# Rounded x and its remainder side by side in the gated feed-forward, and an inverse in halves instead of quarters

## What is computed

```
h   = rms_norm(x, gain)                 # x * gain / sqrt(mean(x^2) + eps), per token
x   = x + 0.5 * (silu(h @ w_gate) * (h @ w_up)) @ w_out      # 1024 -> 2 x 2816 -> 1024
```

```
u = depthwise_conv3(h @ w_up);  x = x + g2 * (silu(u_gate) * u_val) @ w_down
```

## Time and profile before

| | us |
|---|---|
| median of 3 runs | 2930.77 (2929.78 to 2937.19) |
| profiled execution, time | 2935.89 |
| profiled execution, span | 2934.0 |
| PE busy | 2444.5 (83%) |
| PE weight loads busy | 2122.1 (72%) |
| DVE busy | 1165.4 (40%) |
| ACT busy | 1122.3 (38%) |
| POOL busy | 1242.2 (42%) |

### The profile page before, as it was taken

One profiled execution on the slowest core, in us unless ns is written; L12 is line 12 of the kernel. 1 busy time (PEld: TensorE's weight loads), 2 busy tenths in 40 slices (PEclk: granted clock), 3 DMA queues, 4 the chain that ended last, 5 costly groups with the idle time before them and its releaser, 6 DMA issues. The chain is left out here.

```text
span 2934.0 us, 42793 instructions
## 1 busy us (share of the span) xinstructions
PE 2444.5 (83%) x18163; PEld 2122.1 (72%) x18163; DVE 1165.4 (40%) x2067; ACT 1122.3 (38%) x1495; POOL 1242.2 (42%) x356
## 2 busy tenths in 40 slices
PE   5998968877898998977967899699957776887878
PEld 4997845375898998854456799567746556787878
DVE  2112664332210111665242211266756664334990
ACT  4433422434442443322334443456832221533333
POOL 2874510051775775610033577332211110774655
PEclk8999968987999999977987999899967777898998
DMA  4554401431553553500333354321000000553432
GB/s 138 187 175 123 144 1 44 132 125 46 172 180 124 171 182 118 173 29 12 121 113 101 110 180 143 126 76 58 29 1 1 1 1 17 171 172 115 143 123 94
DMA packets 298691, 305.98 MB, mean 104 GB/s; under 512 B 7249, under 2 KB 294461, under 8 KB 298493
## 3 DMA queue, kind: packets, MB, share of 16 engines
q1 hardware_dynamic: 298493, 303.16, 32.1%
HBM read 302.09 MB, written 1.05 MB: 103 GB/s over the span
## 5 line engine op out<-in xcount | busy, mean ns | idle before, releaser
L363 POOL TENSOR_TENSOR slab_lo<-ring,slab_hi 128x2048 fp32r<-128x2048 f32 (+1 forms) x242 | 1096.5, 4540 | 1045.8 <-ACT slab_hi L354 1045.8
L354 ACT CAST slab_hi<-ring 128x2048 fp32r<-128x2048 f32 (+1 forms) x242 | 451.1, 1868 | 639.8 <-PE bank L386 573.4
L384 PE MATMUL bank<-ffn_h_hi,slab_hi 128*128 128x256 f32 x1408 | 403.1, 286 | 24.0 <-DVE ffn_h_lo L426 24.0
L385 PE MATMUL bank<-ffn_h_lo,slab_hi 128*128 128x256 f32 x1408 | 402.2, 286 | 0.0
L386 PE MATMUL bank<-ffn_h_hi,slab_lo 128*128 128x256 f32 x1408 | 402.1, 286 | 0.0
L384 PEld LDWEIGHTS bank<-ffn_h_hi,slab_hi 128*128 128x128 f32 x1408 | 274.5, 195 | 27.2 <-issue 27.2
L385 PEld LDWEIGHTS bank<-ffn_h_lo,slab_hi 128*128 128x128 f32 x1408 | 274.4, 195 | 0.0
L386 PEld LDWEIGHTS bank<-ffn_h_hi,slab_lo 128*128 128x128 f32 x1408 | 274.2, 195 | 0.0
L593 DVE TENSOR_TENSOR hidden<-gate,bank 128x512 f32<-128x512 f32 x44 | 30.2, 687 | 456.8 <-PE bank L386 456.8
L384 PE MATMUL bank<-ffn_hidden_hi,slab_hi 128*128 128x256 f32 x704 | 199.6, 284 | 3.3 <-DVE hidden L593 3.3
L385 PE MATMUL bank<-ffn_hidden_lo,slab_hi 128*128 128x256 f32 x704 | 199.2, 283 | 0.0
(11 more groups left out here) (570 smaller groups left out, 5847.8 us busy)
## 6 DMA issues: line engine op xcount, KB each, us to landing
ring<-in_ffn_w_in SPq DMA_DIRECT2D x88, 1024.0 KB, 5.1
ring<-in_ffn_w_out SPq DMA_DIRECT2D x32, 1024.0 KB, 5.0
ring<-in_w_in SPq DMA_DIRECT2D x30, 1024.0 KB, 5.3
ring<-in_mix_w_in SPq DMA_DIRECT2D x24, 1024.0 KB, 5.4
ring<-in_w_mod SPq DMA_DIRECT2D x24, 1024.0 KB, 5.2
ring<-in_w_up SPq DMA_DIRECT2D x22, 1024.0 KB, 5.1
ring<-in_ffn_w_out SPq DMA_DIRECT2D x16, 768.0 KB, 4.4
ring<-in_mix_w_out SPq DMA_DIRECT2D x8, 1024.0 KB, 5.1
```

Of the source, the lines that this page charges most:

```text
L354: act.copy(self.hi[i % self.PLACES][:, 0:w], K.ring[n % RING][:, 0:w]).then_inc(self.hi_ready, 1)
L363: pool.tensor_tensor(self.lo[i % self.PLACES][:, 0:w], place[:, 0:w], self.hi[i % self.PLACES][:, 0:w].bitcast(F32), ALU.subtract).then_in ...
L384: pe.matmul(out, w[0], act[0], start=start, stop=False)
L385: pe.matmul(out, w[0], act[1], start=False, stop=False)
```

## The change

It has four parts that meet in the diff. In the gated feed-forward, x times gain (without rstd) is rounded, and rounded part and remainder lie side by side in one tile of 512 columns; PE multiplies the rounded weights by both in one matmul and adds the product of weight remainder and rounded x to the first 256 columns. rstd is computed later (`LateNorm`) and DVE multiplies each bank by it and adds the two halves. Each slab takes two whole banks now, so a pair takes four, and the banks change hands every second pair. The output half uses banks in a cycle of eight. Second, POOL begins its splits after the remainder of x. Third, the gains are loaded by a DMA of their own ahead of the slabs. Fourth, the inverse works on two halves of 8 units, level by level, its first transpose is one instruction on copies made by ACT, and DVE and ACT do the widening; scan outputs use one bank.

```diff
+def rounded_both(pe, banks, w, both, first=None):
+    for j in range(2):
+        for k in range(KD):
+            if first is not None and j == 0:
+                first(k)
+            pe.matmul(banks[j][:, :], w[:, k, j * P:(j + 1) * P], both[:, k, :, :].rearrange("p a t -> p (a t)"),
+                      start=(k == 0), stop=False)
+def rest_both(pe, banks, w, both):
+    for j in range(2):
+        for k in range(KD):
+            last = pe.matmul(banks[j][:, 0:T], w[:, k, j * P:(j + 1) * P], both[:, k, 0, :], start=False, stop=(k == KD - 1))
+def out_bank(jj, j):
+    return (2 * jj + j + 4) % 8
...
+class LateNorm:
+    def act_parts(self, act):
+        for k in range(KD):
+            last = act.activation(self.parts.hi[:, k, :], self.x[:, k, :], ACT.Copy, scale=self.gain[:, k:k + 1])
...
+    def dve_parts(self, dve):
...
+            last = dve.scalar_tensor_tensor(self.parts.lo[:, k, :], self.x[:, k, :], self.gain[:, k:k + 1],
+                                            self.parts.hi[:, k, :].bitcast(F32), ALU.mult, ALU.subtract)
+    def dve_squares(self, dve):
+        sq, own = self.K.h, self.K.dve_own
+        own.after(dve, dve.tensor_tensor(sq[:, :, :], self.x[:, :, :], self.x[:, :, :], ALU.mult))
+        for n in (4, 2):
+            own.after(dve, dve.tensor_tensor(sq[:, 0:n, :], sq[:, 0:n, :], sq[:, n:2 * n, :], ALU.add))
+        dve.tensor_tensor(sq[:, 0, :], sq[:, 0, :], sq[:, 1, :], ALU.add).then_inc(self.squared_summed_root, 1)
...
             def _(pool):
+                pool.wait_ge(parts.lo_ready, KD // 2)
                 split.pool(pool)
             def _(act):
-                norm.act(act, between=lambda: split.act(act, 2))
...
+                norm.act_parts(act)
+                split.act(act, 3)
+                norm.act_root(act)
                 for i in range(N):
                     split.act(act, 2 * i + 4)
-                    K.wait_slabs(act, n0 + 2 * i + 1)
-                    if i >= 2:
-                        act.wait_ge(product_ready, i - 1)
-                    act.activation(gate[:, i % 2, :], K.bank[2 * (i % 2)][:, :], ACT.Silu).then_inc(silu_ready, 1)
+                    act.wait_ge(gate_ready, i + 1)
+                    act.activation(gate[:, i % 2, :, :], gate[:, i % 2, :, :], ACT.Silu).then_inc(silu_ready, 1)
                     split.act(act, 2 * i + 5)
                     act.wait_ge(product_ready, i + 1)
-                    act.copy(flat(hidden.hi[:, pair_of(i), :]), whole_hidden[:, i % 2, :]).then_inc(hidden.hi_ready, 1)
+                    hidden.act(act, pair_of(i), whole_hidden[:, i % 2, :, :])
             def _(pe):
...
+                rounded(0)
+                for n in range(2 * N):
+                    if n == 0:
+                        rounded(1)
+                    elif n >= 2:
+                        rounded(n)
+                    pe.wait_ge(split.lo_ready, n + 1)
+                    K.slab_done(rest_both(pe, banks(n), places[n][1], both))
+                    if n == 1:
+                        norm.pe(pe)
+                pe.wait_ge(product_ready, N - 1)
             def _(dve):
...
+                def scaled_sum(odd, part, out):
+                    for j in range(2):
+                        last = dve.tensor_tensor(scaled[part][:, j, :, :], pair(4 * odd + 2 * part + j), norm.all_tokens(2), ALU.mult)
+                    K.dve_own.after(dve, last)
+                    return dve.tensor_tensor(out, scaled[part][:, :, 0, :], scaled[part][:, :, 1, :], ALU.add)
                 for i in range(N + 1):
                     if i < N:
...
+                        scaled_sum(i % 2, 0, gate[:, i % 2, :, :]).then_inc(gate_ready, 1)
+                    if i >= 1:
+                        hidden.dve(dve, pair_of(i - 1), whole_hidden[:, (i - 1) % 2, :, :])
+                    if i < N:
...
+                        K.dve_own.after(dve, scaled_sum(i % 2, 1, up[:, :, :]))
                         dve.wait_ge(silu_ready, i + 1)
...
+                        dve.tensor_tensor(whole_hidden[:, i % 2, :, :], up[:, :, :], gate[:, i % 2, :, :], ALU.mult)\
+                            .then_inc(product_ready, 1)
...
+    def sync_first(self, sync):
+        sync.dma_start(self.first_rows[:, :], self.first_piece).then_inc(self.first_in, 16)
...
+    def act_compact(self, act, g):
+        for i, rows in enumerate(self.GROUPS):
+            act.copy(self.p.compact[rows, 4 * g:4 * g + 4, :], self.lt[rows, 4 * g:4 * g + 4, 32 * i:32 * i + 32])\
+                .then_inc(self.compacted, 1)
...
-        for g, rows in enumerate(self.GROUPS):
-            src = self.lt[rows, :, 32 * g:32 * g + 32].rearrange("p u (b c) -> p c b u", b=2)
-            last = dve.transpose(p.turned[rows, :, :], src)
-        K.dve_own.after(dve, last)
+        dve.wait_ge(self.compacted, 16)
+        K.dve_own.after(dve, dve.transpose(p.turned[:, :, :], p.compact.rearrange("p u (b c) -> p c b u", b=2)))
...
-        self.steps = [(pair * 2 + s, l) for pair in range(2) for l in levels for s in range(2)]
+        self.steps = [(p, l) for l in self.levels for p in range(2)]
...
+        self.pe_first(pe, 0)
+        self.pe_first(pe, 1)
+        for i in range(0, len(self.steps), 2):
+            for step in (i, i + 1):
+                self.pe_second(pe, step)
+                between(step)
+            if i + 2 < len(self.steps):
+                self.pe_first(pe, i + 2)
+                self.pe_first(pe, i + 3)
```

More of the change, by code:

```diff
@@ L537, in _ @@
             def _(sync):
+                if params is not None:
+                    params.sync_first(sync)
                 K.load_slabs(sync, n0 + RING)
@@ L562, in _, with rounded @@
             def _(pe):
[L563 removed]
                 if params is not None:
                     params.pe_first(pe)
[L566 to L573, removed]
[L574 to L578 removed]
+                keep_busy(K, pe, K.bank[4], 3)
+                def rounded(n):
+                    i, part = divmod(n, 2)
+                    places[n] = split.next_rounded(pe)
+                    if n == 3:
+                        pe.wait_ge(norm.squared_summed_root, 3)
+                    if i >= 2:
+                        pe.wait_ge(product_ready, i - 1)
+                    rounded_both(pe, banks(n), places[n][0], both,
+                                 first=(lambda k: pe.wait_ge(parts.lo_ready, k // 2 + 1)) if n == 0 else None)
+                places = {}
+                rounded(0)
[9 more added lines that the diff above has]
+                pe.wait_ge(product_ready, N - 1)
+                if params is not None:
+                    params.pe_rest(pe)
+                ffn_out_pe(K, pe, split, hidden,
+                           lambda jj: pe.wait_ge(product_ready, N) if jj > 1 or params is None else pe.wait_ge(params.first_ready, 2))
             @block.vector
@@ new lines, in pe_first @@
+    def pe_first(self, pe, i):
+        p, l = self.steps[i]
+        pe.wait_ge(self.x_ready, 1 if i < 2 else 2 + i - 1)
+        if l != self.JOIN:
+            pe.wait_ge(self.m_ready, i + 1)
+            last = self.blocks(pe, self.t_bank[p], self.mask[p], self.X(p))
+        else:
+            src, dst = self.joined()
+            for q in range(8):
+                last = pe.matmul(self.t_bank[p][dst, q * CH:(q + 1) * CH], self.lt[src, 8 * p + q, dst],
+                                 self.X(p)[src, q, :], start=True, stop=True)
+        last.then_inc(self.t_ready, 1)
@@ new lines, in pe_second @@
+    def pe_second(self, pe, i):
+        p, l = self.steps[i]
+        pe.wait_ge(self.t_copied, i + 1)
+        pe.wait_ge(self.x_ready, 2 if i < 2 else 2 + i - 1)
+        if l != self.JOIN:
+            if l != self.levels[-1]:
+                self.blocks(pe, self.u_bank[p], self.xt(p), self.T1[p])
+            last = self.blocks(pe, self.v_bank[p], self.T1[p], self.xt(p))
+        else:
+            src, dst = self.joined()
+            for q in range(8):
+                last = pe.matmul(self.v_bank[p][src, q * CH:(q + 1) * CH], self.T1[p][dst, q, :],
+                                 self.xt(p)[dst, q, :], start=True, stop=True)
+        last.then_inc(self.uv_ready, 1)
@@ L1382, in diagonal, with act @@
         for half in self.HALVES:
-            act.copy(self.diag[g][half, :, :], self.lt(g)[half, :, half]).then_inc(self.d_ready, 1)
-    def act(self, act, between=lambda pair: None, first=0):
+            act.copy(self.diag[half, 4 * g:4 * g + 4, :], self.lt[half, 4 * g:4 * g + 4, half]).then_inc(self.d_ready, 1)
+        self.solve.act_compact(act, g)
+    def act(self, act, between=lambda i: None, first=0):
         for g in range(first, 4):
```

279 lines of the change are left out of this document (140 added, 139 removed).

## The result

The changed kernel takes 2949.3 us (median of 9 runs, 2945.0 to 2958.5) against 2933.1 for the kernel before (9 runs, 2929.8 to 2937.2): ratio 1.006, 95% interval 1.0046 to 1.0073. It is 16 us slower, where 2930 and no change were forecast. The profiled execution has a span of 2947.5 us, 13.5 more than that of before.

The account below looks back on a forecast made before the run. PE sets the gated feed-forward's pace before the change, DVE and POOL in turn after it. Feed-forward +45 and inverse -46 sum to -1 us: from the 2930.8 median, 2930, no change; own range 2915 to 2945, whole range 2885 to 2960.

Parts of the forecast that it names:

- +45: Four gated feed-forward stages: longer pairs, with changed starts and ends, cost 13.0 us (second) and 9.7 (first), two of each.
- -46: Inverse of the chunk matrices, both blocks: time saved in us; bounds -30 and -60.
- Part 1: PE in the gated feed-forward: a pair takes 11.1 us instead of 11.52; 18 us saved if PE stayed the bound.
- Part 2: DVE and POOL in a pair: two-SBUF-input operations wait for POOL's splits; pair 12.95 us, 1.43 more; bounds 11.1 and 13.6.
- Part 3: Start and end of a feed-forward stage: first M at 38.7 or 40.2 us, second output columns 7.2 after last M.
- Part 4: Inverse, two in the first block (-17.8 us together), four in the second (-11.7, then three -16.7).
- The steps: Inverse's merged steps: first block 14.1 to 8.7 us (-5.4), first quarter 21.5 to 13.3 (-8.2), later quarters 28.1 to 22.3.
- (d): Rival, inverse: it gives only 30 of its 46 us; 2946 us, chance 0.15.
- (a): Rival, feed-forward pairs: DVE and POOL don't block each other, PE stays the bound, pairs 11.1 us; 2856 us, chance 0.07.
- (b): Rival, feed-forward pairs: POOL's split reaches the ports before the rounding remainder, pairs 13.6 us, +26; 2956 us, chance 0.2.
- (c): Rival: later quarters gain like the first (-14 more), second split overlaps bank products, pairs 12.3 us (-26); 2890, chance 0.18.

Follow-up runs that it names:

- all together: Changed kernel with sums in the banks, POOL's later start, PE kept busy in solves, ACT's copies first: 2865.5 us; with POOL's masks behind the solve too: 2866.4 us.

## Why the prediction was wrong

The forecast was a difference of two large terms, +45 and -46. The first came to +31, the second to -23, and 5.5 us were lost that had no term. That the sum missed by only 15 us is luck: one term was 14 too large, the other 23, and the two errors have opposite signs.

- Part 1, PE's pair of 11.1 us: right. Two kernels in which nothing else holds PE have 11.13 and 11.14. The Trainium skill, "TensorE: Matmul & The Clock Gate", Back-to-back issue gap, gives 131 ns for 512 columns; by the row it was 227, and the pair bears the row out.
- Part 2, the blocking: right in every operation (which two are held up, which two slip through, POOL's two splits back to back), 12.73 instead of 12.95. The run without splits turns it from argued into shown. The Trainium skill, "SBUF — State Buffer", Who interferes with whom, says that a DVE instruction with two SBUF inputs contends with a GpSimd instruction that reads SBUF, and all runs here agree with it. Ten pairs took 126.1 instead of 129.5 us: 0.22 less for each, and the last product ends 1.1 us sooner (3.9 us instead of 5.0). Four times 3.4 is nearly all that the first term was too large by.
- Part 3: right. In the second feed-forward the first M came 39.0 us after ACT's first cast (38.7), in the first 39.4 us after the start (40.2), and PE began the second pair of output columns 7.3 us after the last M (7.2).
- Part 4, ahead of the steps: right in the first block (-0.9 and -2.2 for -1.0 and -2.5) and in the first quarter (-3.1 for -3.5). In the second quarter ACT's 18 copies made the first transposition end 1.9 us later, and the widening gave back 1.3: +0.6 where 0 was put.
- **The step that failed is "The steps" in part 4.** It took "16 matmuls" for a product of eight units and priced them by a row of 32 records. 16 is what the kernel's text has (`blocks`: eight units, two halves), but each of these matmuls leaves two records: the row of 32 was two steps of four units, 16 matmuls in all. So a product of eight units has 32 records and costs twice what was put. PE had the same 320 records to work off as before (448 in a quarter), and was busy already in 12.9 of 14.0 us (18.5 of 21.5). Merging steps saved waits, 1.3 us instead of 5.4 in the first block, 1.5 instead of 8.2 in the first quarter, 0.7 instead of 5.6 in the second. (The -5.6 of a later quarter stands for 28.1 less 22.3, which is 5.8.) Halving the products gives 9.1 us, near the 8.7 of the forecast.
- No term at all: the granted clock behind the first inverse, 7.2 of the 13.5 us between the two profiled executions. It isn't a cost that the change has each time. Of 28 passes traced (two for each kernel), 19 took 282 to 284 us in this stretch and seven took 290 to 291: the changed kernel's first, the second with the sums in the banks (alone, and with POOL's later start), both of the one with ACT's copies first, and one in each of the two kernels with all together. The two passes of the kernel before are among the 19. What decides it, and whether it comes more often in the changed kernel than in the one before, is open.
- Of the rivals, (d) was the nearest, but with 23 of 46 where it had 30. (a), (b) and (c) are refuted: pairs of neither 11.1, 13.6 nor 12.3 us, later quarters not over 8 us shorter each but 1.1, 4.2 and 2.0 (from the ends of their steps).

## What to carry to other kernels

Before a merge of steps is credited with time, count the matmul records of the new step against a row of the old one and look whether PE was idle in it: fewer, larger steps save only the waits between them. A matmul in the text need not be one record in the trace. Where POOL works through a long elementwise operation, DVE's operations are to be written with one input in a bank; more and smaller instructions of that kind beat few with two SBUF inputs. A wait that is shortened on one engine moves its neighbours: ask what now runs beside what. And before a few us between two traces are explained, look at a second pass through the same instructions: here the granted clock alone made 7 us.

## What the runs showed of the hardware

- A DVE operation with a single SBUF tensor (and one scale per partition) was held up too: L1398, a scaling from SBUF to SBUF of 256 elements, 1.47 us for four in the changed kernel, 3.58 beside POOL's masks. The Trainium skill, "SBUF — State Buffer", Who interferes with whom, has it that `tensor_scalar` can enter a 2-port mode and then contends with GpSimd for the pair; the row agrees that it was held, and no run here shows in which mode it ran. Operations that read a bank and one SBUF tensor were never held up, nor those that also write a bank (at most 0.43 us for 256 columns beside POOL's splits, 0.69 for 512).
- The size of the waiting operation didn't matter: one of 12 elements a partition, begun 0.15 us behind POOL's mask of 1.26 us, ended 0.03 us after it, 1.14 us instead of 0.18.
- A plain float32 matmul of 64 x 64 leaves two records in the trace: 320 for the 160 matmuls of an inverse's steps.
- The same 64 records (32 of these matmuls) took 3.68 us at a granted clock of 0.50 and 2.08 at 1.00. Seven filling products ahead of them brought the clock to 0.93 or 1.00 in three of the six inverses that had them, and left it at 0.50 to 0.55 in the other three.
